# Probabilities transposed for two key tiles at a time, with projection pieces and broadcasts directly behind the transposes

## The chip, the cores and the metric

The kernel runs on one core of a Trainium2 chip. The metric is the device time of the whole program in microseconds. A core has TensorE (matmuls into PSUM, eight banks of 128 x 512 f32 values), VectorE, ScalarE, GpSimd and SyncE, each with its own queue of instructions that it runs in order; they wait for each other through semaphores only.

## The reference

One layer of a diffusion backbone over 1024 latent tokens with 256 context tokens, width 1024: a modulated RMS norm and one input projection, Fourier mixing of 256 channels beside grouped-query attention (12 query heads over 4 key heads, head width 64), one output projection, then 16 experts with expert-choice routing. The change touches the attention alone, whose keys are the 1024 latent and the 256 context tokens:

```python
def gqa_block(qi, k_all, v_all):
    s = jnp.einsum('bqkgd,bskd->bkgqs', qi, k_all).astype(jnp.float32) * (HEAD_DIM ** -0.5)
    p = jax.nn.softmax(s, axis=-1).astype(v_all.dtype)
    return jnp.einsum('bkgqs,bskd->bqkgd', p, v_all)

...
    attn_x = latent_attention(qx, kx, vx, kc, vc)
    four_x = fourier_mix(fx, w_four[l])
    x = x + g1 * (jnp.concatenate([four_x, attn_x], axis=-1) @ w_out[l])
    x = x + g2 * expert_choice_ffn(modulate(x, norm_ffn_g[l], sh2, sc2),
                                   w_router[l], w_gate[l], w_up[l], w_down[l])
```

## The kernel before

The program has three stages one behind the other: the input projection and the Fourier part (`nc_phase_a`), attention with output projection and router (`nc_phase_b`), and the experts (`nc_phase_m`). A stage starts when all engines have left the one ahead.

The attention stage goes over eight tiles of 128 query tokens. `schedule` runs nine steps: step 0 (tile 0, no tile ahead of it), step 1, a loop over steps 2 to 7, and step 8 for what is left of the last tile. In a step t each engine runs the same `for i in range(NQ)` over twelve slots. A slot is one query head, and in it `for c in range(NCH + 1)` goes over four places: c = 0, 1, 2 are the key chunks of 512, 512 and 256 keys, c = 3 holds the rest.

In slot i at place c, this happens for head i:

- TensorE writes the scores of chunk c into one of four PSUM banks with two matmuls (L1152, L1153). A bank is free when the exponential four chunks back is done (`exp_done`).
- VectorE takes the maximum of the chunk (L1049, `mx`). At c = 2 it reduces the three (L1053) and writes the bias `nb` (L1054), from which the exponentials of this head wait in the next slot.
- ScalarE computes the exponential of chunk c of head i - 1 into `pr` (L979), which frees the score bank.

Three heads share one key head and form a group. When a group's probabilities are there, ten key tiles of 128 keys ("items") are turned and multiplied with the values, in the three slots behind it: four in the first of them, three and three in the next (`items`). An item k takes this way:

- TensorE transposes three 128 x 128 blocks (one per head) into bank `PTB + k % 2` (L1168). It waits for the remainder of item k - 2, which read the same bank (`lo_done`), and for items 0, 4 and 8 of a group for the exponential of that chunk.
- ScalarE copies the 128 x 384 block in reduced precision into `pth` (L995), VectorE subtracts it from the original and writes the remainder `ptl` (L1058).
- TensorE multiplies the values with both (`times`, L1128 and L1129, the first and the second product), two items later: behind the transposes of item k stands `times(k - 2)`. The last two items of a group are multiplied in the next slot that is a multiple of three, the flush slot (0, 3, 6, 9).

In a flush slot at c = 0 the group is finished too: ScalarE copies one half of the sum (`oth`, L986 or L988), VectorE adds the halves (`osum`, L1066), TensorE broadcasts the reciprocals of the denominators by a matmul of `ones` with `diag` (L1190), ScalarE copies the broadcast (`rbc`, L999), and GpSimd scales and writes `mix` (L930).

Slots 4 and 5 hold the output projection of the tile ahead (`out_part`, L1137): eight matmuls each, every one in two passes, two matmuls behind each place c. Behind slots 8 and 9 stand four transposes of the normed tile (L1206), behind slot 10 the router product (L1213), whose maximum VectorE takes (L1105, L1106) for ScalarE's exponential (L1019), behind slot 11 a small transpose of the affinities (L1217), which ScalarE copies (L1024).

Before the change there is one item at each place c: `its[c]`.

Of the kernel before, what the change touches and what calls it, by code (L numbers as in the profile page):

```python
# [8 lines left out]
P = 128  # L9
# [5 lines left out]
REP = NQ // NKV  # L15
# [760 lines left out]
def nc_phase_b(nc, ctx, sem, sb, a, K, psum, ident, ones, rows, aff, cand, eps_c, ks, vs, y_t,  # L776
# [39 lines left out]
    KT = TS  # L816
    NT = KT * NKV
    PTB, OB, MB = 4, 6, 7
# [38 lines left out]
    def items(i, prev, cur):  # L857
# [5 lines left out]
        return [KT * g + k for k in range(lo, hi)]  # L863

    def behind(t, i, prev, cur):

        if i == 0:
            return (t - 1, NQ - 1) if prev else None
        return (t, i - 1) if cur else None

    with nc.Block() as block:
# [90 lines left out]
        def _(act):  # L962
            def step(t, prev, cur):
                use = use_numbers(prev, cur)
                fl = flushes(prev, cur)
                for i in range(NQ):
                    its = items(i, prev, cur)
                    ex = behind(t, i, prev, cur)
                    for c in range(NCH + 1):
# [11 lines left out]
                        if c == 0 and i in fl:  # L981
# [5 lines left out]
                            else:  # L987
                                act.activation(oth[HD:P, :], psum[0:HD, OB, 0:REP * P], ACT.Copy).then_inc(s["oth_done"], 1)  # L988
                        if c < len(its):
                            k = its[c]  # L990
                            n = NT * t + k
# [38 lines left out]
        def _(dve):  # L1030
            def step(t, prev, cur):
# [11 lines left out]
                for i in range(NQ):  # L1043
                    its = items(i, prev, cur)
                    for c in range(NCH + 1):
# [4 lines left out]
                        if cur and c == NCH - 1:  # L1050
# [3 lines left out]
                            dve.tensor_scalar(nb[:, i:i + 1], mx[:, i, 3:4], -SCALE, None, ALU.mult).then_inc(s["nb_done"], 1)  # L1054
                        if c < len(its):
                            k = its[c]
                            dve.wait_ge(s["hi_done"], NT * t + k + 1)
# [57 lines left out]
        def _(pe):  # L1115
            def step(t, prev, cur):
# [15 lines left out]
                def misc_free(name):  # L1132
                    after(pe, s["misc_free"], misc(t, use[name]))
# [7 lines left out]
                for i in range(NQ):  # L1141
                    its = items(i, prev, cur)
                    for c in range(NCH + 1):
# [10 lines left out]
                        if c == 0 and i in fl:  # L1154
                            k0 = KT * (fl[i] + 1)
                            times(k0 - 2)
                            times(k0 - 1)
                        if c < len(its):
                            k = its[c]
                            n = NT * t + k  # L1160
# [9 lines left out]
                            ins.then_inc(s["t_done"], 1)  # L1170
                            if kt >= 2:
                                times(k - 2)
                        if prev and cur and i in (4, 5):
# [9 lines left out]
                            if c == NCH:  # L1183
                                ins.then_inc(s["misc_mm"], 1)
                        if c == 0 and i in fl:
                            G = 4 * t + fl[i]

                            pe.wait_ge(s["diag_done"], G + 1)
                            misc_free(f"R{i}")
                            pe.matmul(psum[:, MB, 0:REP * P], ones[:, :], diag[fl[i] % 2][:, :, :].rearrange("p r n -> p (r n)"),  # L1190
                                      start=True, stop=True).then_inc(s["misc_mm"], 1)
                    if not cur and i in (4, 5):
# [470 lines left out]
```

## Time and profile before

| | us |
|---|---|
| median of three runs | 2033.14 |
| lowest and highest | 2031.74, 2034.86 |
| the profiled execution, its own time | 2035.89 |
| span of the profiled execution | 2033.3 |
| PE busy in the span | 1856.9 (91%) |
| DVE busy in the span | 1614.0 (79%) |
| ACT busy in the span | 1303.5 (64%) |

The rows below come from one profiled execution; times are us from the start of its span. PE is TensorE, DVE VectorE, ACT ScalarE, POOL GpSimd. A timeline row gives the start, the length from the first start to the last end, the engine, the line of the kernel, what it writes and reads, and how many instructions are merged (x3). Matmuls overlap in the array, so a row's length is longer than what it adds to a queue of them; the distance of two starts, or of two ends, is what an instruction costs. In brackets stands how long the engine was idle before it, and who ended that. PEclk is the granted clock as a share of 2.4 GHz.

### The profile page before, as it was taken

To read this page: it belongs to the slowest core of one execution; us is meant where nothing else is said; L and a number is where in the kernel's file an instruction comes from. 1 tells how busy PE (TensorE), PEld (TensorE's weight loads), DVE (VectorE), ACT (ScalarE), POOL (GpSimd) and SP (SyncE) were. 2 spreads that over 40 slices of the span, in tenths; PEclk is the share of its full clock that TensorE was granted. 3 is DMA by queue.
4 is the path that set the end of the run, shared out by engine and by line. 5 is a ranking of instruction groups with operands and counts; after the bars stand their busy time and mean duration, and the time that the engine had idled before them with its cause. 6 is when DMAs were issued, how large, how long until landed. Compare 5 with 4: busy or idle time off the path is not lost.

```text
span 2033.3 us, 28027 instructions
## 1 busy us (share of the span) xinstructions
PE 1856.9 (91%) x8691; PEld 1462.4 (72%) x8691; DVE 1614.0 (79%) x2070; ACT 1303.5 (64%) x1921; POOL 290.0 (14%) x294
## 2 busy tenths in 40 slices
PE   6998869899899889719999999999999999999996
PEld 3776647666666666517888888888888888888884
DVE  5777547766766767487989998999899989998996
ACT  4444347666766766416777777777777777777774
POOL 0233221110111111101101100110011001110113
PEclk8999879999999999958999999999999999999998
DMA  8556480210110120039999999999999999999996
GB/s 353 172 151 170 109 228 28 63 41 22 62 44 28 52 62 10 31 120 365 396 394 390 376 377 402 389 381 370 405 386 384 368 404 386 373 384 398 380 379 245
DMA packets 108034, 512.28 MB, mean 252 GB/s; under 512 B 12064, under 2 KB 36040, under 8 KB 57296
## 3 DMA queue, kind: packets, MB, share of 16 engines
q1 hardware_dynamic: 101792, 489.11, 63.7%
q0 software_dynamic: 4752, 17.30, 3.2%
q10 hardware_dynamic: 1440, 5.24, 0.7%
q8 instruction: 26, 0.43, 0.1%
q14 instruction: 24, 0.20, 0.0%
HBM read 481.71 MB, written 27.28 MB: 250 GB/s over the span
## 4 chain that ended last, share of the span: by engine, by line
PE 54%; DVE 2%; DMA 1%; issue 0%; ACT 0%; POOL 0%
PE banks L1599 34%; PE banks L1624 17%; PE banks L1611 1%; PE banks L1580 1%; DVE topi L1458 1%; DVE top L1456 1%; DVE cand L1459 1%; DMA xe<-h_scratch,icol 0%; DVE raw L1554 0%; DMA out<-raw 0%; DVE ysc L1518 0%; DVE ysc L1561 0%; ACT d_hi L1421 0%; POOL out L1381 0%; DVE x_lo L1484 0%
## 5 line engine op out<-in xcount | busy, mean ns | idle before, releaser
L1490 DVE TENSOR_TENSOR w_lo<-raw,w_hi 128x2048 fp32r<-128x2048 f32 x256 | 574.8, 2287 | 67.9 <-ACT w_hi L1399 67.9
L1399 ACT ACTIVATE w_hi<-raw 128x2048 fp32r<-128x2048 f32 x256 | 470.8, 1919 | 10.5 <-DMA raw<-in_w_exp 10.4
L1599 PE MATMUL banks<-w_hi,x_hi 128*128 128x512 f32 x1024 | 406.2, 397 | 1.4 <-DVE x_lo L1484 1.4
L1599 PE MATMUL banks<-w_hi,x_lo 128*128 128x512 f32 x1024 | 400.6, 391 | 0.0
L1599 PE MATMUL banks<-w_lo,x_hi 128*128 128x512 f32 x1024 | 400.1, 391 | 0.0
L1498 DVE TENSOR_TENSOR d_lo<-raw,d_hi 128x1024 fp32r<-128x1024 f32 x256 | 296.2, 1218 | 1.5 <-ACT d_hi L1421 1.4
L1421 ACT ACTIVATE d_hi<-raw 128x1024 fp32r<-128x1024 f32 x256 | 258.1, 1060 | 38.5 <-DMA raw<-in_w_exp 24.7
L1058 DVE TENSOR_TENSOR ptl<-banks,pth 128x384 fp32r<-128x384 f32 x320 | 176.6, 555 | 66.8 <-ACT pth L995 61.5
L995 ACT ACTIVATE pth<-banks 128x384 fp32r<-128x384 f32 x320 | 156.9, 490 | 109.3 <-PE banks L1168 101.1
L1599 PEld LDWEIGHTS banks<-w_hi,x_lo 128*128 128x128 f32 x1024 | 192.9, 188 | 40.7
L1599 PEld LDWEIGHTS banks<-w_hi,x_hi 128*128 128x128 f32 x1024 | 193.2, 189 | 39.7 <-DVE x_lo L1484 1.8
L1049 DVE TENSOR_REDUCE mx<-banks 128x1 f32<-128x512 f32 (+1 forms) x288 | 170.8, 594 | 63.2 <-PE banks L1153 62.7
L1599 PEld LDWEIGHTS banks<-w_lo,x_hi 128*128 128x128 f32 x1024 | 193.4, 189 | 38.1
L1405 ACT ACTIVATE sil<-banks 128x512 f32<-128x512 f32 x64 | 38.3, 598 | 251.5 <-PE banks L1599 251.5
L979 ACT ACTIVATE pr<-banks,nb 128x512 f32<-128x512 f32 (+1 forms) x288 | 177.0, 615 | 23.3 <-DVE nb L1054 21.6
L1152 PE MATMUL banks<-ks,qt 128*128 128x512 f32 (+1 forms) x288 | 144.1, 500 | 34.9 <-ACT pr L979 28.1
L1168 PE MATMUL banks<-ident,pr 128*128 128x128 f32 x960 | 163.3, 280 | 7.2 <-DVE ptl L1058 4.4
L1330 POOL TENSOR_TENSOR carry<-carry 128x1 f32<-128x1 f32 x32 | 37.8, 1181 | 920.8 <-DVE ysc L1518 583.5
L1624 PE MATMUL banks<-d_hi,h_hi 128*128 128x512 f32 x512 | 158.8, 392 | 2.6 <-DVE h_lo L1504 2.6
L1624 PE MATMUL banks<-d_lo,h_hi 128*128 128x512 f32 x512 | 158.3, 391 | 0.0
L1624 PE MATMUL banks<-d_hi,h_lo 128*128 128x512 f32 x512 | 158.2, 391 | 0.0
L1168 PEld LDWEIGHTS banks<-ident,pr 128*128 128x128 f32 x960 | 117.0, 142 | 47.6 <-DVE ptl L1058 18.0
(213 smaller groups left out, 2768.4 us busy)
## 6 DMA issues: line engine op xcount, KB each, us to landing
raw<-in_w_exp SPq DMA_DIRECT2D x384, 1024.0 KB, 8.0
a_ring<-in_w_mod SPq DMA_DIRECT2D x32, 512.0 KB, 5.0
qt<-q_scratch SPq DMA_DIRECT2D x64, 192.0 KB, 3.6
a_slot<-in_w_mod SPq DMA_DIRECT2D x8, 1024.0 KB, 12.0
a_w_raw<-in_w_in SPq DMA_DIRECT2D x3, 2048.0 KB, 30.2
q_scratch<-a_qst SPq DMA_DIRECT2D x16, 384.0 KB, 3.9
a_xt<-in_x ACTq DMA_DIRECT2D x8, 512.0 KB, 6.1
xr<-in_x SPq DMA_DIRECT2D x8, 512.0 KB, 4.0
```

The source lines that it names most:

```text
L979: act.activation(pr[(h // 3 % 2) * 3 + h % 3][:, lo:hi], psum[:, (NCH * h + c) % 4, 0:hi - lo], ACT.Exp, bias=nb[:, h:h + 1], scale=SCALE, ...
L995: act.activation(pth[:, k % 4, :], psum[:, PTB + k % 2, 0:REP * P], ACT.Copy).then_inc(s["hi_done"], 1)
L1049: ins = dve.tensor_reduce(mx[:, i, c:c + 1], psum[:, (NCH * i + c) % 4, 0:hi - lo], AX, ALU.max)
L1058: dve.tensor_tensor(ptl[:, k % 4, :], psum[:, PTB + k % 2, 0:REP * P], pth[:, k % 4, :].bitcast(F32), ALU.subtract).then_inc(s["lo_done"], 1)
L1152: pe.matmul(o, qt[:, i, 0, :], ks[:, i // 3, lo:hi], start=True, stop=False)
L1168: ins = pe.transpose(psum[:, PTB + k % 2, r * P:(r + 1) * P], pr[(g % 2) * 3 + r][:, kt * P:(kt + 1) * P], ident[:, :])
L1399: act.activation(w_hi[which][c][:, :], raw[which][c][:, :], ACT.Copy).then_inc(s["hi_done"], 1)
L1421: act.activation(d_hi[k][:, :], raw[2][k // 2][:, k % 2 * D:(k % 2 + 1) * D], ACT.Copy).then_inc(s["d_hi_done"], 1)
L1490: dve.tensor_tensor(w_lo[which][c][:, :], raw[which][c][:, :], w_hi[which][c][:, :].bitcast(F32), ALU.subtract).then_inc(s["lo_done"], 1)
L1498: dve.tensor_tensor(d_lo[k][:, :], raw[2][k // 2][:, k % 2 * D:(k % 2 + 1) * D], d_hi[k][:, :].bitcast(F32), ALU.subtract).then_inc(s["d_l ...
L1599: i = pe.matmul(psum[:, 2 * (j % 2) + which, :], x_[par][:, k, :], w_, start=(k == 0 and w_ is hi and x_ is x_hi), stop=(k == KD - 1 and x ...
L1624: i = pe.matmul(psum[:, Y + h, :], x_[:, k, :], w_[k][:, h * 512:(h + 1) * 512], start=(j == 0 and k == 0 and x_ is h_hi and w_ is d_hi), ...
```

## The change

A helper `batch(its, c)` gives two items at c = 0 and the other two (or one) at c = 2, and none at c = 1 and 3. TensorE, ScalarE and VectorE all use it. On TensorE the loop over the items now holds the transposes alone; behind it stand the broadcast of a flush slot (ahead of the projection now, no longer behind it), the two projection matmuls of the place, and only then the products of the items two back. In the diff the hunk at 986 is ScalarE's, the one at 1052 VectorE's, the rest TensorE's.

```diff
+    def batch(its, c):
+
+        return its[c:c + 2] if c % 2 == 0 else []
...
@@ -986,8 +990,7 @@
-                        if c < len(its):
-                            k = its[c]
+                        for k in batch(its, c):
...
@@ -1052,8 +1055,7 @@
-                        if c < len(its):
-                            k = its[c]
+                        for k in batch(its, c):
...
@@ -1155,8 +1157,7 @@
-                        if c < len(its):
-                            k = its[c]
+                        for k in batch(its, c):
                             n = NT * t + k
                             g, kt = k // KT, k % KT
...
                             ins.then_inc(s["t_done"], 1)
-                            if kt >= 2:
-                                times(k - 2)
+                        if c == 0 and i in fl:
+                            G = 4 * t + fl[i]
+
+                            pe.wait_ge(s["diag_done"], G + 1)
+                            misc_free(f"R{i}")
+                            pe.matmul(psum[:, MB, 0:REP * P], ones[:, :], diag[fl[i] % 2][:, :, :].rearrange("p r n -> p (r n)"),
+                                      start=True, stop=True).then_inc(s["misc_mm"], 1)
                         if prev and cur and i in (4, 5):
...
                             ins = out_part(j, (2 * c, 2 * c + 1), c == 0, c == NCH)
                             if c == NCH:
                                 ins.then_inc(s["misc_mm"], 1)
-                        if c == 0 and i in fl:
-                            G = 4 * t + fl[i]
-
-                            pe.wait_ge(s["diag_done"], G + 1)
-                            misc_free(f"R{i}")
-                            pe.matmul(psum[:, MB, 0:REP * P], ones[:, :], diag[fl[i] % 2][:, :, :].rearrange("p r n -> p (r n)"),
-                                      start=True, stop=True).then_inc(s["misc_mm"], 1)
+                        for k in batch(its, c):
+                            if k % KT >= 2:
+                                times(k - 2)
```

How the rows of a slot stand now is seen in step 1; the loop of steps 2 to 7 has the same order. On TensorE, slot 9 (a flush slot), behind its two flush products, before:

```order
L1168 MATMUL banks<-ident,pr 128x128 x3
L1190 MATMUL banks<-diag,ones 128x384
L1152 MATMUL banks<-ks,qt 128x512
L1153 MATMUL banks<-ks,qt 128x512
L1168 MATMUL banks<-ident,pr 128x128 x3
L1152 MATMUL banks<-ks,qt 128x256
L1153 MATMUL banks<-ks,qt 128x256
L1168 MATMUL banks<-ident,pr 128x128 x3
L1128 MATMUL banks<-pth,vs 128x384
L1129 MATMUL banks<-ptl,vs 128x384
L1168 MATMUL banks<-ident,pr 128x128 x3
L1128 MATMUL banks<-pth,vs 128x384
```

and in the changed kernel, where the new lines are L1169 (transposes), L1177 (broadcast), L1154 and L1155 (scores), L1130 and L1131 (products):

```order
L1169 MATMUL banks<-ident,pr 128x128 x6
L1177 MATMUL banks<-diag,ones 128x384
L1154 MATMUL banks<-ks,qt 128x512
L1155 MATMUL banks<-ks,qt 128x512
L1154 MATMUL banks<-ks,qt 128x256
L1155 MATMUL banks<-ks,qt 128x256
L1169 MATMUL banks<-ident,pr 128x128 x6
L1130 MATMUL banks<-pth,vs 128x384
L1131 MATMUL banks<-ptl,vs 128x384
L1130 MATMUL banks<-pth,vs 128x384
L1131 MATMUL banks<-ptl,vs 128x384
```

The transposes of two items stand together, the broadcast behind six of them and not behind three, the third score (128 x 256) directly behind the second, and the products in one run at the end.

On ScalarE, slots 9 and 10 of the same step, from the flush slot's `oth` to the copy of slot 10, before:

```order
L988 ACTIVATE oth<-banks 64x384
L995 ACTIVATE pth<-banks 128x384
L999 ACTIVATE rbc<-banks 128x384
L979 ACTIVATE pr,den<-banks,nb 128x512
L995 ACTIVATE pth<-banks 128x384
L979 ACTIVATE pr,den<-banks,nb 128x256
L995 ACTIVATE pth<-banks 128x384 x2
L1006 ACTIVATE h2t<-banks 128x512
L979 ACTIVATE pr,den<-banks,nb 128x512
L995 ACTIVATE pth<-banks 128x384
L979 ACTIVATE pr,den<-banks,nb 128x512
L995 ACTIVATE pth<-banks 128x384
```

and in the changed kernel (L983 the exponential, L998 the copy into `pth`, L1002 `rbc`):

```order
L992 ACTIVATE oth<-banks 64x384
L998 ACTIVATE pth<-banks 128x384 x2
L1002 ACTIVATE rbc<-banks 128x384
L983 ACTIVATE pr,den<-banks,nb 128x512
L983 ACTIVATE pr,den<-banks,nb 128x256
L998 ACTIVATE pth<-banks 128x384 x2
L1009 ACTIVATE h2t<-banks 128x512
L983 ACTIVATE pr,den<-banks,nb 128x512
L998 ACTIVATE pth<-banks 128x384 x2
L983 ACTIVATE pr,den<-banks,nb 128x512
L983 ACTIVATE pr,den<-banks,nb 128x256
L998 ACTIVATE pth<-banks 128x384
```

Two copies into `pth` stand ahead of the second exponential where there was one; the second and the third exponential stand together, and the copies of place 2 and 3 behind them. The change of VectorE is the same for `ptl` among the maxima.

In slots 4 and 5 the row of a place was transposes x3, two products, projection x2; it is now transposes (of one or two items), projection x2, then the products.

## Rows read from the trace of the kernel before

**Rows 1.** windows of the attention stage and of one steady tile; columns as printed

```profile
core 0: us, PE busy (x) PEld busy (x) DVE busy (x) ACT busy (x) POOL busy (x), PEclk, DMA share, GB/s
266.30:861.70 595.40, 529.66 (x2671) 380.38 (x2671) 408.82 (x963) 378.20 (x1013) 95.59 (x99) 0.97 0.19 55
542.50:614.40 71.90, 65.02 (x337) 46.88 (x337) 51.38 (x121) 47.27 (x128) 10.77 (x12) 1.00 0.14 44
```

**Rows 2.** what TensorE waited for in the tile 542.5 to 614.4 us

```profile
engine line waited for: us in total, times, longest us
PE banks L1152 <- ACT pr L979: 3.6, 9, 0.7
PE banks L1217 <- DVE lg L1110: 1.5, 1, 1.5
...
PE banks L1168 <- DVE ptl L1058: 0.5, 2, 0.3
```

**Rows 3.** timeline, TensorE, slot 4: transposes, products, projection, scores

```profile
start us, us, engine line op out<-in xcount [idle before <-releaser]
...
567.35 0.49 PE L1168 MATMUL banks<-ident,pr 128*128 128x128 f32 x3
567.60 0.42 PE L1128 MATMUL banks<-pth,vs 128*128 128x384 f32 x1
567.86 0.33 PE L1129 MATMUL banks<-ptl,vs 128*128 128x384 f32 x1
568.03 3.60 PE L1137 MATMUL banks<-wout,mix 128*128 128x512 f32 x8
...
571.69 0.40 PE L1153 MATMUL banks<-ks,qt 128*128 128x512 f32 x1
```

**Rows 4.** timeline, slot 2: biases, exponentials, copy, a score, last maximum

```profile
623.83 0.15 DVE L1054 TENSOR_SCALAR nb<-mx 128x1 f32<-128x1 f32 x1
...
624.02 0.69 ACT L979 ACTIVATE pr<-banks,nb 128x512 f32<-128x512 f32 x1 [0.52 <-DVE nb L1054]
...
624.70 0.48 ACT L995 ACTIVATE pth<-banks 128x384 fp32r<-128x384 f32 x1
...
624.85 0.50 PE L1152 MATMUL banks<-ks,qt 128*128 128x512 f32 x1 [0.35 <-ACT pr L979]
...
625.07 0.69 ACT L979 ACTIVATE pr<-banks,nb 128x512 f32<-128x512 f32 x1
...
626.95 0.41 DVE L1049 TENSOR_REDUCE mx<-banks 128x1 f32<-128x256 f32 x1
...
627.59 0.15 DVE L1054 TENSOR_SCALAR nb<-mx 128x1 f32<-128x1 f32 x1
```

**Rows 5.** timeline, slot 3, a flush slot, the same view

```profile
629.90 0.49 ACT L999 ACTIVATE rbc<-banks 128x384 f32<-128x384 f32 x1
...
629.95 0.56 DVE L1058 TENSOR_TENSOR ptl<-banks,pth 128x384 fp32r<-128x384 f32 x1 [1.15 <-ACT pth L995]
...
630.28 0.68 ACT L979 ACTIVATE pr<-banks,nb 128x512 f32<-128x512 f32 x1
...
631.11 0.39 PE L1152 MATMUL banks<-ks,qt 128*128 128x256 f32 x1 [0.45 <-ACT pr L979]
...
631.33 0.28 PE L1153 MATMUL banks<-ks,qt 128*128 128x256 f32 x1
...
632.31 0.41 DVE L1049 TENSOR_REDUCE mx<-banks 128x1 f32<-128x256 f32 x1
...
632.45 0.55 PE L1168 MATMUL banks<-ident,pr 128*128 128x128 f32 x3 [0.16 <-DVE ptl L1058]
```

**Rows 6.** timeline, end of the tile, ScalarE in slot 11 and TensorE

```profile
608.96 0.27 ACT L1019 ACTIVATE lg<-banks,st 128x16 f32<-128x16 f32 x1 [1.95 <-DVE st L1106]
...
613.83 0.28 PE L1217 MATMUL banks<-ident,lg 128*16 128x128 f32 x1 [1.46 <-DVE lg L1110]
```

**Rows 7.** timeline, TensorE in the last step, slot 0

```profile
835.60 0.55 PE L1168 MATMUL banks<-ident,pr 128*128 128x128 f32 x3 [0.57 <-DVE ptl L1058]
...
836.34 4.46 PE L1137 MATMUL banks<-wout,mix 128*128 128x512 f32 x10
```

**Rows 8.** windows: a tile with a clock drop, and the drop

```profile
469.20:542.50 73.30, 66.48 (x337) 48.20 (x337) 51.48 (x121) 47.23 (x128) 10.74 (x12) 0.98 0.14 43
469.20:472.60 3.40, 3.40 (x10) 2.93 (x11) 0.69 (x1) 1.51 (x5) 0.00 (x0) 0.50 0.63 194
```

## The prediction

> **What bounds the kernel now.** I read the windows first, to see what the change can reach; then the list of what TensorE waited for; then the timeline of one tile, slot by slot. The changed loops are the attention stage, 595.40 of 2033.3 us at a granted clock of 0.97, and one steady tile of it is 71.90 us, in which TensorE is busy 65.02, VectorE 51.38 and ScalarE 47.27 [rows 1]. No engine is full, yet TensorE's listed waits come to a few us only: scores that wait for an exponential are 3.6, a transpose that waits for a remainder 0.5, and the small transpose at the tile's end 1.5 [rows 2]. There are two kinds of slot (a slot is one query head). Slots 4 and 5 hold the projection and are full on TensorE. The other ten run as a ring through three engines: scores, maximum on VectorE, exponential on ScalarE, which frees the score bank of the next head. In the ring a handover counts, not a busy share, and there the change moves work.
>
> **The unit costs.** Three transposes of one key tile are 0.33 us: they start 0.11 apart, since the x3 row is 0.49 long where a single one is 0.27. Transposes and the first product start 0.51 apart from the second product, so the first product takes 0.18; the second takes 0.17 up to the projection. Eight passes of the projection take 0.43 each ((3.60 - 0.59) / 7), so 3.44, and from their start to the second score half are 3.66: the first half takes 0.22 [rows 3]. A key tile thus costs 0.68, a score of 512 columns 0.47, one of 256 0.24, and a three-tile slot 3 x 0.68 + 2 x 0.47 + 0.24 = 3.22 of TensorE, before as after: the change adds and removes no matmul.
>
> **Part 1: fewer changes of kind.** Transposes, products and projection follow each other in longer runs. What a change costs is the difference of 0.18 and 0.17 above, 0.01; out of the projection it is 0.22 against 0.23 for the second half of a score, nothing [rows 3]. Twenty changes fewer a tile are at most 0.2 us a tile, 1.6 in all. I take 0 and keep 1.6 in the range.
>
> **Part 2: the middle slots.** ScalarE now copies two key tiles between its first and second exponential, not one. From one head's bias to the next, before: 627.59 - 623.83 = 3.76 [rows 4]. After, the chain is bias to exponential 0.19 (624.02 - 623.83), exponential 0.68 (624.70 - 624.02), two copies at 0.37 (625.07 - 624.70), second exponential to the third score 0.83 (as 624.85 - 624.02), score to its maximum 0.55 (a score that starts after a wait: 631.33 + 0.28 - 631.11 = 0.50, and 0.05 to VectorE), maximum to bias 0.64 (627.59 - 626.95): 3.63 [rows 4, 5]. That is 0.13 better, but the second transpose of the pair needs the remainder of the last tile of the slot ahead, which now comes just behind it, and by the same units this costs some 0.1 of the copy. I take 0 for a middle slot, from -0.13 to +0.1.
>
> **Part 3: the flush slots (0, 3, 6, 9).** The broadcast now stands behind six transposes, so it ends 0.33 later, ScalarE's copy of it too (629.90), the second exponential (630.28) and the third score (631.11), which so ends at 631.94 where it was 631.33 + 0.28 = 631.61. What covers it is VectorE: from 629.95 it works off remainder, sum, maximum, remainder and only at 632.31 takes the last maximum [rows 5]. The same four now stand in another order with the same sum, so the bias stays, and 632.31 - 631.99 = 0.32 of cover is left. If that were gone, each 0.33 would count, 4 x 0.33 = 1.3 a tile. Against it, the transposes of the fourth tile no longer wait for a remainder that has just been begun (632.45, 0.16 idle): two pairs back to back, 0.66, products 0.70 and the next score 0.47 behind 631.94 end at 633.77, where the sum of before is the same within 0.1. ScalarE's last copy comes 0.3 earlier, but the next slot is held by TensorE or VectorE. I take 0.
>
> **Part 4: the projection slots.** They move from products, then projection to projection, then products. TensorE is full there, 3.22 + 2 x 3.44 = 10.1 a slot, and every waiting partner (copy, remainder) has 1.7 us of projection as cover. 0.
>
> **Part 5: the router's end of the tile.** In slot 10 the third score did not wait before; with two copies ahead of the second exponential it waits some 0.3 (the 0.37 of a copy less what TensorE had as slack). Everything behind it on TensorE moves by this: the router product, then VectorE's negated maximum, ScalarE's L1019 (608.96, idle 1.95 until then) and, queued behind it on ScalarE, the exponentials of slot 11; then the small transpose at 613.83, for which TensorE already idles 1.46, and the first exponential of the next tile [rows 6]. Nothing lies beside this chain. I take +0.3 a tile, from 0 to +0.37, for seven tiles +2.1.
>
> **Part 6: first tile and last step.** The first tile has neither router nor projection and gets its slots at 0, -0.3 if a second pair of transposes falls into the wait for its first broadcast; I take -0.2. In the last step there are no scores to fill the waits: a transpose waits 0.57 for a remainder before the projection starts at 836.34 [rows 7]. With pairs, and with the copies ahead of the last exponentials, the units above let that projection start some 0.8 earlier, and slots 1 and 2 lose 0.2 to 0.3 each of such waits. I take -1.2, from 0 to -1.8.
>
> **The sum.** 2.1 - 0.2 - 1.2 = +0.7. For the profiled execution (2035.9, its span 2033.3) that is 2036.6; the median of the runs shown is 2033.14, 2.8 under the profiled one, so I forecast **2033.8**. On the error of the terms: seven tiles at -0.5 to +0.6 and the ends at -1.8 to 0 give 2028 to 2038 for this case by itself.
>
> **The rivals.** (A, 0.57) the forecast: what the pairs give back at one handover they take at the next.
> (B, 0.15) **slower: the flush is not covered.** Place: the third score of slots 0, 6 and 9, where VectorE has less to work off than in slot 3. It decides once the last maximum waits for its score and not for VectorE, that is once the score comes over 0.32 later than in [rows 5]. Price 4 x 0.33 = 1.3 a tile, 7 x 1.3 = 9, on top of the forecast: 2043; half of the slots: 2038. For it: the score is late by just the size of the cover. Against it: VectorE's four operations keep their sum.
> (C, 0.17) **faster: the small waits go.** TensorE's 3.6 + 0.5 of waits for exponentials and remainders [rows 2] are on its queue; if products behind a pair and projection ahead of products cover a quarter, that is 1.0 a tile, 7 us, with the last step 8: 2025. Against it: the third score gets a new wait in seven slots.
> (D, 0.05) **the change of kind costs.** The second product starts 0.26 behind the first when that follows transposes, 0.17 elsewhere. Read as a penalty of 0.09, 20 x 8 x 0.09 = 14 us would go: 2019. Against it: the first product then starts 0.25 behind the transposes, less than their 0.33; the two together leave 0.01 [rows 3].
> (E, 0.06) **the clock.** In two of the seven steady tiles the granted clock was at its lower level (0.50, 1.2 GHz) for 3.40 us behind the idle of the tile's end, and such a tile took 73.30 us, not 71.90 [rows 1, 8]. The change adds an idle of some 0.3 to 0.5 us ahead of the third score in most slots and moves more of it next to that end. If all seven tiles drop, 5 x 1.4 = 7 us: 2041.
> The Trainium skill, in "TensorE: Matmul & The Clock Gate", section "A second HAM failure mode: psum-queue depth-cycling", says that short idles of the PE between groups of matmuls that cycle through PSUM banks make the clock swing between its two levels. By that rule E is the likely case; the trace disagrees so far, as a tile with nine such waits ran at 1.00 [rows 1, 2].
> That the change does not do what it says is no rival: the order shows the pairs.
>
> **How the numbers follow.** About 0.2%, 4 us, is what a measurement of this kernel can tell from no change: faster is below 2029, slower above 2037.2. Faster: C and D nearly whole, 0.20. Slower: two thirds of B, E, and the upper end of A, 0.19. Within: 0.61. The range 2027 to 2040 reaches into C and B and leaves out D, E and the far half of B, some 0.2.
>
> **What would show it.** Right: a steady tile of 71.9 to 72.3 us; a wait of the third score for an exponential in slots 1, 2, 7, 8, 10, 11; transposes that wait for no remainder; the last maximum of a flush slot waiting for VectorE's own queue; L1019 0.3 later in its tile; the projection of the last step 0.8 earlier. Wrong: an idle of VectorE ahead of that last maximum (B), a tile under 71.3 us (C), a first product behind transposes that shortens the slot by more than the waits did (D), lower clock in more than three tiles (E).

## The result

| | before | after |
|---|---|---|
| median of 7 runs, us | 2032.08 | 2037.52 |
| lowest and highest | 2030.83, 2034.86 | 2036.38, 2042.10 |
| the profiled execution, its own time and span | 2035.89, 2033.3 | 2040.48, 2038.5 |

The ratio is 1.0029, with a 95% interval of 1.0017 to 1.0041: the change makes the kernel slower by 5.4 us. The forecast was 2033.8, the range 2027 to 2040.

First the windows of after: one undisturbed tile, the next one with a clock drop (a stretch at the lower granted clock, 0.50), and that drop by itself. They answer to [rows 1, 8].

```profile
core 0: us, PE busy (x) PEld busy (x) DVE busy (x) ACT busy (x) POOL busy (x), PEclk, DMA share, GB/s
543.10:615.70 72.60, 65.11 (x337) 47.41 (x337) 51.54 (x121) 46.35 (x128) 10.76 (x12) 1.00 0.14 43
615.70:689.40 73.70, 66.48 (x337) 48.97 (x337) 51.58 (x121) 46.62 (x128) 10.74 (x12) 0.98 0.15 43
682.70:686.10 3.40, 3.40 (x13) 3.11 (x12) 2.02 (x5) 2.93 (x9) 0.00 (x0) 0.50 0.00 0
```

At full clock a tile takes 72.60 us where it took 71.90, and the engines are busy as before (TensorE 65.11 against 65.02). The 0.7 us (0.8 by the finer ruler below) is therefore waiting, not work. What TensorE waited for in that tile, beside [rows 2]:

```profile
engine line waited for: us in total, times, longest us
PE banks L1154 <- ACT pr L983: 5.0, 7, 0.8
PE banks L1219 <- DVE lg L1112: 1.2, 1, 1.2
...
PE banks L1169 <- ACT pr L983: 0.2, 1, 0.2
```

The transposes no longer wait for a remainder (0.5 before, no line now), but the scores wait 5.0 us for exponentials and not 3.6, in seven longer waits and not nine. The best ruler for where the loss sits is the start of the bias row (`nb`), once in each slot: L1054 before, L1057 after. The distance from each bias to the next, in one undisturbed tile, for the two kernels and for the experiments told below (us; column "0" is from slot 0's bias to slot 1's, and so on):

| kernel | 0 | 1 | 2 | 3 | 4 | 5 | 6 | 7 | 8 | 9 | 10 | 11 |
|---|---|---|---|---|---|---|---|---|---|---|---|---|
| before | 4.22 | 3.75 | 5.36 | 7.12 | 10.23 | 8.28 | 5.06 | 4.53 | 6.01 | 4.92 | 5.54 | 6.84 |
| after | 4.35 | 3.80 | 5.39 | 7.23 | 10.25 | 8.33 | 4.93 | 4.64 | 5.91 | 5.05 | 5.83 | 6.96 |
| e3_pairs_only | 4.35 | 3.80 | 5.38 | 7.24 | 10.07 | 8.33 | 4.93 | 4.63 | 5.91 | 5.04 | 5.83 | 6.92 |
| e2_order_only | 4.23 | 3.75 | 5.36 | 7.12 | 10.58 | 8.29 | 5.07 | 4.53 | 6.01 | 4.93 | 5.53 | 6.85 |
| e1_copies_single | 4.77 | 4.17 | 5.36 | 7.38 | 10.24 | 8.61 | 4.87 | 4.53 | 6.15 | 5.21 | 5.37 | 8.67 |
| c1_copies_paired | 5.14 | 4.51 | 6.19 | 7.16 | 10.23 | 9.17 | 6.12 | 4.64 | 6.88 | 5.81 | 6.70 | 7.81 |
| h1_late | 3.76 | 3.85 | 6.19 | 6.43 | 10.24 | 8.97 | 4.58 | 4.85 | 6.48 | 4.43 | 6.12 | 7.59 |
| g1_pairs_5679 | 4.22 | 3.76 | 5.36 | 7.11 | 10.07 | 8.34 | 4.93 | 4.64 | 5.90 | 5.16 | 5.53 | 6.84 |

The undisturbed tiles repeat these to 0.02 in nearly every column; the last column of e1 has a clock drop in it. Columns 2, 5, 8 and 11 end at the bias of a flush slot (3, 6, 9 and the next tile's 0). So after loses 0.8 us a tile: +0.29 in column 10; 0.11 to 0.13 each in columns 0, 3, 7, 9 and 11; it wins 0.13 and 0.10 in columns 6 and 8. Seven tiles are 5.6. The last step, from the last bias to the experts' first row, is 0.54 shorter (42.64, now 42.10; f1 and f2 below repeat both), and the expert stage is the same (1161.0 and 1160.9). The first tile went from 61.61 to 59.64, but it lies anywhere between 58.5 and 67.9 in the kernels below, so nothing is read from it. 7 x 0.8 - 0.5 = 5.1 us of the measured 5.4.

**A middle slot.** Timeline of after, slot 2, beside [rows 4]:

```profile
552.64 0.15 DVE L1057 TENSOR_SCALAR nb<-mx 128x1 f32<-128x1 f32 x1
552.83 0.69 ACT L983 ACTIVATE pr<-banks,nb 128x512 f32<-128x512 f32 x1
552.84 0.56 DVE L1060 TENSOR_TENSOR ptl<-banks,pth 128x384 fp32r<-128x384 f32 x1
552.93 1.07 PE L1169 MATMUL banks<-ident,pr 128*128 128x128 f32 x6
553.51 1.02 ACT L998 ACTIVATE pth<-banks 128x384 fp32r<-128x384 f32 x2
554.42 0.68 ACT L983 ACTIVATE pr<-banks,nb 128x512 f32<-128x512 f32 x1
555.25 0.38 PE L1154 MATMUL banks<-ks,qt 128*128 128x256 f32 x1
556.44 0.15 DVE L1057 TENSOR_SCALAR nb<-mx 128x1 f32<-128x1 f32 x1
```

The remainder of the slot ahead ends at 552.84 + 0.56 = 553.40. Six transposes in a row that wait for nothing are 0.82 long (slot 5, below); these are 1.07, because the second three stand behind that remainder. So the second copy is late too: two copies from 553.51 to the second exponential at 554.42 are 0.91, where two at 0.37 would be 0.74. Those 0.17 added to the predicted chain of 3.63 make 3.80, which is what is measured: 556.44 - 552.64.

**A flush slot.** Timeline of after, slot 3, beside [rows 5]:

```profile
558.94 1.02 DVE L1060 TENSOR_TENSOR ptl<-banks,pth 128x384 fp32r<-128x384 f32 x2 [1.14 <-ACT pth L998]
559.21 0.49 ACT L1002 ACTIVATE rbc<-banks 128x384 f32<-128x384 f32 x1
...
560.42 0.39 PE L1154 MATMUL banks<-ks,qt 128*128 128x256 f32 x1 [0.79 <-ACT pr L983]
...
561.83 0.15 DVE L1057 TENSOR_SCALAR nb<-mx 128x1 f32<-128x1 f32 x1
562.59 0.96 PE L1169 MATMUL banks<-ident,pr 128*128 128x128 f32 x6
```

The third score waits 0.79 (0.45 before), as forecast, and it costs nearly nothing (column 2: +0.03; column 5: +0.05). It is covered by VectorE's queue: in all four flush slots the last two maxima stand in one row of 1.01 to 1.04 us, with no idle before it.

**Three more columns, by their rows.** They do not all have slot 2's cause.

- Column 9 has the chain of slot 2. Behind the flush slot's second pair the transposes of the normed tile start 0.47 behind the bias (0.23 before), and so the first exponential comes 1.60 behind it (1.36 before); 1.60 + 0.68 + 0.74 + 0.83 + 0.55 + 0.64 = 5.04, measured 5.05.
- In column 3 it is TensorE, which runs through. The first score starts 0.30 behind the bias (0.23 before), the pair's transposes behind it are 0.96 long, not 0.82 (the last row above), and the projection starts 1.56 behind the bias (1.45 before): the whole 0.11.
- In column 7 it is VectorE. The last copy of the slot ahead now ends 0.16 behind the bias, so VectorE's first remainder starts 0.20 behind it (0.10 before), and from there VectorE has no idle up to the next bias.

**The router's end.** Timeline of after, slots 10 and 11, beside [rows 6]:

```profile
606.98 0.39 PE L1154 MATMUL banks<-ks,qt 128*128 128x256 f32 x1 [0.50 <-ACT pr L983]
608.00 1.85 PE L1215 MATMUL banks<-wrt,h2t 128*128 128x16 f32 x16
610.29 0.27 ACT L1022 ACTIVATE lg<-banks,st 128x16 f32<-128x16 f32 x1 [1.95 <-DVE st L1108]
612.81 0.38 PE L1154 MATMUL banks<-ks,qt 128*128 128x256 f32 x1 [0.57 <-ACT pr L983]
615.15 0.28 PE L1219 MATMUL banks<-ident,lg 128*16 128x128 f32 x1 [1.17 <-DVE lg L1112]
```

The third score of slot 10 now waits 0.50, where it waited for nothing, and the router product stands behind it on TensorE. It starts at 608.00, 0.17 ahead of slot 10's bias (608.17); before, it started 0.57 ahead (606.67 and 607.24). ScalarE idles 1.95 for it as before, and the first exponential of slot 11 comes 2.39 behind the bias instead of 1.98, which is +0.41. Slot 11 itself is 0.12 shorter from there (3.44 for 3.56), so column 10 rises by 0.29. In column 11 the last remainder waits for its copy, which ends only at 614.17, and VectorE's work on the affinities is queued behind it: +0.12.

### The profile page after: what moved, and what is told of

It reads as the page before. It is cut to its first block, busy times and chain, and to the rows that moved or that the text cites. A ratio compares the mean times of both kernels' runs of the same rounds, so it can differ in the third digit from the quotient of the medians.

```text
span 2038.5 us, 28027 instructions
## 1 busy us (share of the span) xinstructions
PE 1862.6 (91%) x8691; PEld 1469.9 (72%) x8691; DVE 1617.1 (79%) x2070; ACT 1296.8 (64%) x1921; POOL 298.2 (15%) x294
## 4 chain that ended last, share of the span: by engine, by line
PE 54%; DVE 2%; DMA 1%; issue 0%; ACT 0%; POOL 0%
PE banks L1601 34%; PE banks L1626 17%; PE banks L1613 1%; PE banks L1582 1%; DVE topi L1460 1%; DVE top L1458 1%; DVE cand L1461 1%; DMA xe<-h_scratch,icol 0%; DVE raw L1556 0%; DMA out<-raw 0%; DVE ysc L1520 0%; DVE ysc L1563 0%; ACT d_hi L1423 0%; POOL out L1383 0%; DVE x_lo L1486 0%
## 5 line engine op out<-in xcount | busy, mean ns | idle before, releaser
L998 ACT ACTIVATE pth<-banks 128x384 fp32r<-128x384 f32 x320 | 146.7, 491 | 134.9 <-PE banks L1169 131.1
L1060 DVE TENSOR_TENSOR ptl<-banks,pth 128x384 fp32r<-128x384 f32 x320 | 167.7, 553 | 60.9 <-ACT pth L998 56.4
L1332 POOL TENSOR_TENSOR carry<-carry 128x1 f32<-128x1 f32 x32 | 51.5, 1608 | 910.9 <-DVE ysc L1520 583.5
L983 ACT ACTIVATE pr<-banks,nb 128x512 f32<-128x512 f32 (+1 forms) x288 | 176.0, 620 | 11.3 <-DVE nb L1057 9.1
L1154 PE MATMUL banks<-ks,qt 128*128 128x512 f32 (+1 forms) x288 | 137.9, 479 | 46.0 <-ACT pr L983 36.8
L1169 PE MATMUL banks<-ident,pr 128*128 128x128 f32 x960 | 147.5, 282 | 4.1 <-ACT pr L983 2.6
L1169 PEld LDWEIGHTS banks<-ident,pr 128*128 128x128 f32 x960 | 113.7, 144 | 28.4 <-DVE ptl L1060 9.6
```

Source lines behind the costliest of these rows:

```text
L983: act.activation(pr[(h // 3 % 2) * 3 + h % 3][:, lo:hi], psum[:, (NCH * h + c) % 4, 0:hi - lo], ACT.Exp, bias=nb[:, h:h + 1], scale=SCALE, ...
L998: act.activation(pth[:, k % 4, :], psum[:, PTB + k % 2, 0:REP * P], ACT.Copy).then_inc(s["hi_done"], 1)
L1060: dve.tensor_tensor(ptl[:, k % 4, :], psum[:, PTB + k % 2, 0:REP * P], pth[:, k % 4, :].bitcast(F32), ALU.subtract).then_inc(s["lo_done"], 1)
L1154: pe.matmul(o, qt[:, i, 0, :], ks[:, i // 3, lo:hi], start=True, stop=False)
L1169: ins = pe.transpose(psum[:, PTB + k % 2, r * P:(r + 1) * P], pr[(g % 2) * 3 + r][:, kt * P:(kt + 1) * P], ident[:, :])
```

## The experiments

Some expectations call the theories by letter. H is the handover: two copies ahead of the second exponential hold up the third score. O is TensorE's own order: the transposes of a pair wait for remainders, and the products come late. K is the clock: more drops at the tile's end are the loss (rival E of the prediction). All kernels but c1 (two executions) and e5 (one) were timed in several rounds beside before. The medians of before in the three sets of runs were 2033.71, 2032.49 and 2031.94, so ratios are compared, not medians.

### e1_copies_single: pairs on TensorE alone

```diff
-                        for k in batch(its, c):
+                        for k in its[c:c + 1]:
```

(on after, in the loops of ScalarE and VectorE)

> TensorE's order as in the changed kernel; ScalarE's copies and VectorE's remainders one at a place, as before. Theory H (the loss is the second copy ahead of the second exponential, which the third score waits for): a middle slot's chain falls to 0.19 + 0.68 + 0.37 + 0.83 + 0.55 + 0.64 = 3.26 us, a steady undisturbed tile from 72.7 us to 71.9 or less, down to 71; the kernel within 0.2% of before or faster. Theory O (TensorE's own order loses: transposes of a pair wait for remainders, products come late): the tile stays at 72.7 and the kernel 0.3% slower. Theory K (the clock at the tile's end is the larger part): tile 72.7, and more than two tiles with a drop.

Measured: 2054.32, ratio 1.0107 (1.0088 to 1.0125), so four times the loss of after. The simple form of H, that the pair of copies is the cost and single copies would take it away, is refuted: slot 2 (column 1) takes 4.17, where 3.26 was expected. Timeline of e1, slot 2 of a tile (636.85 is slot 1's bias, 641.02 slot 2's), and what TensorE waited for between 350 and 830 us:

```profile
636.85 0.15 DVE L1057 TENSOR_SCALAR nb<-mx 128x1 f32<-128x1 f32 x1
636.95 0.56 DVE L1060 TENSOR_TENSOR ptl<-banks,pth 128x384 fp32r<-128x384 f32 x1
637.57 0.55 PE L1169 MATMUL banks<-ident,pr 128*128 128x128 f32 x3 [0.67 <-DVE ptl L1060]
638.64 0.40 PE L1154 MATMUL banks<-ks,qt 128*128 128x512 f32 x1
639.31 0.69 DVE L1052 TENSOR_REDUCE mx<-banks 128x1 f32<-128x512 f32 x1 [0.52 <-PE banks L1155]
641.02 0.15 DVE L1057 TENSOR_SCALAR nb<-mx 128x1 f32<-128x1 f32 x1
...
PE banks L1154 <- ACT pr L983: 23.0, 38, 0.8
PE banks L1169 <- DVE ptl L1060: 8.6, 25, 0.7
```

With single remainders on VectorE, the second transposes of a pair wait for a remainder that VectorE only starts behind its bias (636.95). They and the products behind them stand ahead of the second score, which comes at 638.64, and VectorE idles 0.52 for it. The change moved a score back behind two items, and only the matching order on the other engines makes that bearable. Part of e1's loss is the clock, though: its profiled execution had a drop behind six of its seven steady tiles. Columns 0 to 10 hold none and add up to 66.66, where before has 65.02, so at least 1.6 us a tile, 11 in all, are the order's own.

### c1_copies_paired: pairs on ScalarE and VectorE alone

```diff
-                        if c < len(its):
-                            k = its[c]
+                        for k in batch(its, c):
```

(on before, in ScalarE and VectorE; TensorE as before)

> The other half of e1: TensorE's order as before the change, ScalarE's copies and VectorE's remainders in pairs. Now the second copy ahead of the second exponential waits for transposes that stand behind the second score. Chain of a middle slot: bias to exponential 0.19, exponential to second score 0.83, score 0.74, transposes 0.33 and 0.05 to ScalarE, copy 0.37, second exponential to third score 0.83, score to maximum 0.55, maximum to bias 0.64: 4.5 us where it was 3.76. Matched-order theory (a pair costs little only if all three engines take it together): slots 1, 2, 7, 8, 10, 11 and the flush slots lose 0.3 to 0.8 each, a tile of 74 to 77 us, the kernel 1 to 2% slower than before. If the second copy in itself were the whole cost, the tile would be that of the changed kernel, 72.7.

Measured: 2109.92, ratio 1.0381 (1.0355 to 1.0408). The mechanism came out to the digit in the middle slot (4.51 in column 1, 4.5 expected), but every column except 3, 4 and 7 loses 0.8 to 1.2, more than the 0.3 to 0.8 expected, so the undisturbed tile was 80.4, not 74 to 77. TensorE's waits in one tile, and one of them in the timeline:

```profile
PE banks L1154 <- ACT pr L983: 13.3, 13, 1.7
...
584.23 0.39 PE L1154 MATMUL banks<-ks,qt 128*128 128x256 f32 x1 [1.71 <-ACT pr L983]
```

ScalarE's second exponential stands behind a copy whose transposes TensorE has queued behind the second score. Half of the change on either side costs 1.1% and 3.8%, both halves together 0.3%. Here too clock drops have a share, up to 13.7 us long in the profiled execution (483.5 to 497.2 us); the 8.5 us that an undisturbed tile loses are some 60 of the 78 us.

### e2_order_only and e5_broadcast_only: the order without the pairs

e2, on after:

```diff
-        return its[c:c + 2] if c % 2 == 0 else []
+        return its[c:c + 1]
```

> One key tile at a place on all engines; only the broadcast and the projection pieces stand ahead of the products. H: nothing changes, a steady tile 71.9 us, ratio 1.000. O: a tile of 72.1 to 72.4. If changes of kind on TensorE cost anything, the tile is shorter than 71.8.

Measured: 2034.59, ratio 1.0008 (0.9996 to 1.0020). All columns are as before but column 4, 10.23 to 10.58. Timeline of e2 there (slot 5), and the waits between 350 and 830 us:

```profile
572.83 0.69 DVE L1091 TENSOR_TENSOR x<-banks,rows 128x512 f32<-128x512 f32 x1 [2.95 <-PE banks L1139]
572.84 0.49 PE L1169 MATMUL banks<-ident,pr 128*128 128x128 f32 x3
573.57 1.12 PE L1139 MATMUL banks<-wout,mix 128*128 128x512 f32 x2 [0.24 <-DVE x L1091]
...
PE banks L1139 <- DVE x L1091: 1.5, 6, 0.2
```

The projection of slot 5 writes the bank that VectorE is still reading for slot 4's half. Before, two products stood in between and covered most of that reading (how much is told at e3). e5 is e2 with the products back ahead of the projection, and only the broadcast early:

> One key tile at a place; only the broadcast stands ahead of the products, the projection pieces behind them as before. In e2 with both moved, slot 5 took 10.58 us from bias to bias and not 10.24, and its first projection matmul waited for VectorE's reading of the bank. If that wait is the whole cost of the order, slot 5 is back at 10.24 here and the tile at 71.87; if the broadcast has a share, it stays above.

Its only execution took 2031.5, and column 4 is 10.24 again, the other columns as before. So the early broadcast costs nothing, and the early projection costs 0.34.

### e3_pairs_only and e4_single_10_11: the pairs without the order, and without the router's slots

e3, on after, TensorE:

```diff
                             ins.then_inc(s["t_done"], 1)
+                        for k in batch(its, c):
+                            if k % KT >= 2:
+                                times(k - 2)
...  (projection, then the broadcast, as before the change)
-                        for k in batch(its, c):
-                            if k % KT >= 2:
-                                times(k - 2)
```

> Pairs on all engines, but the products directly behind the pair, and broadcast and projection where they stood before. H: the whole loss stays, a steady tile 72.7 us, ratio 1.003, as the changed kernel. O with the late products as its cause: tile back to 71.9 to 72.2.

Measured: 2038.53, ratio 1.0032 (1.0020 to 1.0043), which can't be told from after's. An undisturbed tile is 72.45. Every column is after's, except column 4, which is 10.07: the pairs win 0.16 there, and in after the early projection gives 0.18 back. So the late products of after, the second half of theory O, are not its loss. The rows of after in slot 5, then two projection rows of before and one of e3:

```profile
572.79 0.82 PE L1169 MATMUL banks<-ident,pr 128*128 128x128 f32 x6
573.52 1.98 PE L1139 MATMUL banks<-wout,mix 128*128 128x512 f32 x4
...
572.77 0.69 DVE L1091 TENSOR_TENSOR x<-banks,rows 128x512 f32<-128x512 f32 x1 [2.95 <-PE banks L1139]
...
572.66 1.98 PE L1137 MATMUL banks<-wout,mix 128*128 128x512 f32 x4
575.62 1.88 PE L1137 MATMUL banks<-wout,mix 128*128 128x512 f32 x4
...
574.33 1.88 PE L1139 MATMUL banks<-wout,mix 128*128 128x512 f32 x4
```

The projection of after starts at 573.52, 0.06 behind the end of VectorE's reading (572.77 + 0.69), as in e2. The kernel before already waited for that bank: its first projection row in the slot starts 0.23 behind the second product (572.43 to 572.66), where the next one starts 0.17 behind (575.45 to 575.62), and it is 1.98 long, not 1.88. That is a wait of 0.06 + 0.10 = 0.16. In e3 the row starts 0.17 behind the product and is 1.88 long: four products now stand in between, and the wait is gone. In after it starts 0.73 behind six transposes and in e2 0.73 behind three, where 0.65 and 0.32 are the distances without a wait (0.32 later in the same slot of both), and 0.10 more on the row's length makes 0.18 and 0.51. Added to e3's 10.07 these three waits are 10.23, 10.25 and 10.58: what the four kernels differ by in column 4 is this one wait.

e4, on after:

```diff
-        return its[c:c + 2] if c % 2 == 0 else []
+        return its[c:c + 1] if i in (10, 11) else its[c:c + 2] if c % 2 == 0 else []
```

> The changed kernel with slots 10 and 11 taken one key tile at a place on all three engines. My term for the router's end of the tile was +0.3 us; the changed kernel's trace shows bias to bias +0.29 from slot 10 to 11 and +0.12 from 11 to the next tile. H: both go, a steady tile of 72.3 us and the router's exponential 0.3 us earlier in its tile; kernel 0.1% faster than the changed one. K: no change but for the number of clock drops.

Measured: 2036.73, ratio 1.0015 (1.0005 to 1.0025); the tile is 72.36. Column 10 goes back from 5.83 to 5.54 and column 11 from 6.96 to 6.83, and column 9 rises from 5.05 to 5.17. So pairs in these two slots cost 0.29 + 0.13 - 0.12 = 0.30 a tile, and the other 0.5 of after's loss lies elsewhere.

### f1_before_fill and f2_after_fill: is it the clock?

```diff
+                    if prev and cur and i == 11:
+                        for _ in range(10):
+                            pe.transpose(psum[:, MB, 2 * P:3 * P], ident[:, :], ident[:, :])
```

(ten idle transposes into an unused part of a bank, just ahead of the small transpose at the tile's end; f1 on before, f2 on after)

> The kernel before with ten more transposes of the identity (1.1 us) ahead of the small transpose at a tile's end, into columns that nobody reads. Theory K (an idle of 1.46 us there lets the clock fall in some tiles, 1.3 to 1.5 us each): no clock drop between 340 and 830 us, tiles of 71.9 us throughout, 2 to 3 us less than before where its profile had two drops. Rival: the drops come from the whole stretch around the tile's end, and stay.

> The changed kernel with the same ten transposes. If K is the larger part of its loss, the four drops of its profile go (5 to 6 us) and it comes out at the time of before. If the handovers are the loss (H), an undisturbed tile stays at 72.7 us and against the filled kernel before it stays 7 x 0.8 - 0.5 = 5 us behind.

Measured: f1 2031.29, ratio 0.9993 (0.9984 to 1.0003); f2 2036.11, ratio 1.0027 (1.0018 to 1.0037). The gain of 2 to 3 us expected of f1 does not stand out of the noise. The windows from 340 to 830 us, the steady tiles, of f1, before, after and f2, in this order:

```profile
340.00:830.00 490.00, 451.32 (x2361) 326.82 (x2361) 349.28 (x824) 319.68 (x860) 73.46 (x82) 1.00 0.13 42
340.00:830.00 490.00, 444.85 (x2284) 320.32 (x2283) 347.38 (x817) 318.76 (x857) 73.42 (x82) 0.99 0.14 42
340.00:830.00 490.00, 441.72 (x2245) 322.34 (x2244) 343.98 (x806) 309.67 (x844) 73.39 (x82) 0.99 0.14 42
340.00:830.00 490.00, 447.17 (x2330) 328.04 (x2331) 345.95 (x812) 310.26 (x851) 73.28 (x82) 1.00 0.14 42
```

In these single executions before had two drops and f1 none, after four and f2 one, yet f2 stays 4.8 us above f1, close to the 5.1 of seven tiles at 0.8 less the last step. The undisturbed tiles are 71.9 and 72.65 as without it. The drops are real (a tile with one is 1.0 to 1.5 longer), but they are not the loss.

### h1_late and g1_pairs_5679: can a part of the gain be kept?

h1, on before (all engines): a slot of three items puts the second and third at c = 2.

```diff
-                        if c < len(its):
-                            k = its[c]
+                        for k in place(its, c, i, prev, cur):    # three items: {0: its[0:1], 2: its[1:3]}
```

> The kernel before, but in slots with three key tiles the second and third are taken together at place 2, behind the third score, and none at place 1; one copy stands ahead of the second exponential and two behind the third. If what ScalarE has between the first and the second exponential sets the distance from bias to bias (refined H), slot 2's falls from 3.76 towards 3.35 (VectorE's own sum), a tile by 0.5 to 1.0 us, the kernel by 3 to 7 us. If pairs lose in themselves (their transposes and products hold the next score back on TensorE, theory O), the tile is longer than 71.9 as with the change.

Measured: 2043.64, ratio 1.0057 (1.0040 to 1.0074). Columns 0, 3, 6 and 9 fall by 0.46 to 0.69, but columns 2, 5, 8, 10 and 11 rise by 0.47 to 0.83, and slot 2's (column 1), which the expectation had falling towards 3.35, rises to 3.85. The falls are the columns that begin at a flush slot's bias, and four of the five rises are those that end at one: the items that a slot puts off are left to the next flush slot, as far as the columns tell.

g1, on e3: pairs in slots 5, 6, 7 and 9 and in the last step alone.

```diff
+        if i in (5, 6, 7, 9) or not cur:
+            return its[c:c + 2] if c % 2 == 0 else []
+        return its[c:c + 1]
```

> Pairs only in slots 5, 6, 7 and 9 and in the last step, products directly behind them, broadcast and projection in their old places. In the trace of the pairs alone the distance from bias to bias was 0.17 shorter in slot 5, 0.14 from 6 to 7, 0.10 into slot 9, and the last step 0.5. If these gains are those slots' own, a tile takes 71.5 us and the kernel 0.1% less than before; if they only give back what earlier slots had lost, 71.9.

Measured: 2031.22, ratio 0.9994 (0.9985 to 1.0004). The gains of columns 4, 6 and 8 (0.16, 0.13, 0.11) are there, and columns 5, 7 and 9 give back 0.06, 0.11 and 0.24; the tile is 71.87, as before, and not the 71.5 of gains that stay.

### g2_pairs_5_fill: what is left that pays

g1 with `if i == 5 or not cur`, and the ten transposes of f1.

> Pairs only in slot 5 and in the last step, products behind them, order otherwise as before, and the ten transposes at the tile's end. Slot 5 alone gained 0.17 in e3 and g1, and the slots behind it gave it back where they too held pairs. If a single pair slot keeps its gain: tiles of 71.7 us without drops, 0.1 to 0.15% less than before. If the wait moves to slot 6 anyway: 71.87, and what is left is the filler's 0.05%.

Measured: 2028.59, ratio 0.9985 (0.9975 to 0.9994), the only kernel faster than both. Its undisturbed tile and the granted clock:

```profile
539.90:611.60 71.70, 65.95 (x347) 48.05 (x347) 51.31 (x121) 47.15 (x128) 10.75 (x12) 1.00 0.14 44
```

Column 4 is 10.07 and column 5 is 8.30, so 0.15 a tile is kept: it is the wait for the bank (e3) that is gone. No tile up to 848 us has a drop. Which share is the pair's and which the filler's was not tried apart: the filler alone (f1) was too small for a measurement, and a pair in slot 5 alone was not run without it (g1 has pairs in three more slots).

## Why the forecast came out as it did

The time lies inside the range, and inside the 2028 to 2038 that the forecast's case had by itself. But the change came out slower than the 0.2% (0.29%, its interval from 0.17%), which was given 0.19, and the size of the working was off: +5.4 against +0.7. That the time fell inside the ranges is owed to their width more than to the sum. By parts:

**Part 1, changes of kind: right.** e2 has fewer changes of kind and the same columns but one. Rival D is gone.

**Part 2, middle slots: mis-sized, and that is the largest miss.** The text worked out the chain of 3.63 and, beside it, "some 0.1" for the second transposes, which wait for the last remainder; it then wrote 0 because the two seemed to cancel. The term measured 0.17, and the two together +0.05 in slot 2, not -0.13. The other four columns that lost by 0.11 to 0.13 (0, 3, 7, 9) were not worked out at all: the one slot looked at stood for ten, and of the three whose rows were read only column 9 has slot 2's chain. The sum of columns 0, 1, 3, 6, 7, 8 and 9 is +0.30 a tile, 2.1 in all.

**Part 3, flush slots: right.** The third score waits 0.79, 0.34 longer than before, and VectorE covers it; columns 2 and 5 rise by 0.03 and 0.05. Rival B's median for half of the slots, 2038, is what was measured, but not by its mechanism.

**Part 4, projection slots: wrong in its reason.** "1.7 us of projection as cover" looked at copies and remainders that wait. It did not ask which partner the projection itself waits for: the bank that VectorE reads for the first half. The early projection costs 0.34 with single items (e2) and 0.18 with pairs; the pairs' own win of 0.16, which is the wait of before for the same bank, hid it, so the column shows +0.02 and the 0 looked right. That was luck.

**Part 5, router's end: right in mechanism, under-sized.** Columns 10 and 11 rise by 0.41 (forecast 0.3, bound 0.37), in two places: the router product 0.40 later against the bias, and the affinities' way to the small transpose 0.12 longer. Slot 11's shorter chain takes 0.12 back. Times seven, 0.41 is 2.9, not 2.1.

**Part 6, the last step: half.** The projection started 0.56 earlier, not 0.8, and slots 1 and 2 won nothing, where 0.2 to 0.3 each had been put; in all -0.54, not -1.2. Timeline of after, last step, beside [rows 7]:

```profile
839.87 1.01 PE L1169 MATMUL banks<-ident,pr 128*128 128x128 f32 x6 [0.20 <-DVE ptl L1060]
...
841.65 0.59 PE L1139 MATMUL banks<-wout,mix 128*128 128x512 f32 x1
```

The wait of 0.57 for a remainder shrank to 0.20, but the six transposes are 1.01 long: the pair waits inside itself, as in slot 2.

**Rivals.** B needed an idle of VectorE ahead of the last maximum of a flush slot; there is none. C needed the small waits to go. Those for remainders did; those for exponentials grew from 3.6 to 5.0. E is excluded as the cause by f1 and f2; its sign, drops in more than three tiles, did not come either (four drops in three tiles). The Trainium skill's rule on clocks that swing with short idles ("TensorE: Matmul & The Clock Gate", section "A second HAM failure mode: psum-queue depth-cycling") is not borne out in these rows: in f2 TensorE had as many such waits as after, and the steady tiles ran at 1.00 but for one drop. How many drops an execution has varies besides: e5, with before's columns, had three in its steady tiles (at 532.9, 611 and 823 us), two of them at another place in the tile than before's, so two against four is no evidence by itself.

What stays open: what column 0's 0.13 consists of. Its first score starts 0.50 behind the bias (0.23 before), but how that and VectorE's queue share the loss was not worked out, and no experiment takes the pairs of a flush slot away by themselves.

## What to carry to other kernels

Where three in-order engines hand work round a ring, the order is a property of all three: changing it on one (at least 1.6 us a tile) or two (8.5) costs two to ten times what changing it on all three does (0.8). A gain read off one slot must be followed into the next slot before it is booked, since there it is mostly given back; a term of 0.1 us that sits in ten slots of seven tiles is as large as anything else in the sum. Before a matmul is put earlier, ask what it waits for itself (here, the reader of its own bank), and not only who waits for it.

## What the hardware showed that was not expected

The lower clock level (0.50, 1.2 GHz) comes for some 3.4 us at a time, and at two places of a tile. Before's two drops (469.2 and 687.6 us) come behind the idle of 1.46 us at the tile's end. Of after's four only the one at 689.5 does; the other three (535.9, 682.6 and 757.7) begin in slot 10 within 0.3 us of the end of the router product, sixteen matmuls of 16 columns that keep TensorE busy for 1.85 us (680.70 to 682.55 for the second), and TensorE had no idle there: its last wait before, 0.50 us, ended 1.0 us ahead of the product. The one drop of f2 (752.8) stands there too. So the clock fell at the end of a row in which TensorE was busy, and not only behind idles.

Ten transposes fill 1.1 of the 1.46 us of idle at the tile's end. f1, f2 and g2, which have them, show no drop behind the end of a steady tile. But g1 and h1, without them, show none either, so that the filler prevents drops is not shown. The wait that is left for the small transpose in one tile of f1:

```profile
PE banks L1220 <- DVE lg L1110: 0.4, 1, 0.4
```

The Trainium skill says in "TensorE: Matmul & The Clock Gate", section "Part 4: PE-mode transpose", that transposes don't count as activity for the clock as matmuls do; no run here decides it, since executions without the filler had no drops at the tile's end either. The opposite case is e1, where the profiled execution had a drop behind six of its seven steady tiles (at 475.0, 550.1, 625 us and so on, one tile of some 75 us apart); what makes its drops so regular was not tried.

A score that waits for the exponential of its own bank starts 0.83 us behind that exponential's start, in before and after alike (624.02 to 624.85 in [rows 4] for the second; 554.42 to 555.25 in after), so what moves an exponential moves the score by the same amount.
